# Sums of squares over each head's outputs: from one float32 product to two rounded ones, one gate panel later

## The chip, the cores and the metric

The kernel runs on one core of a Trainium2 chip. The metric is the device time of one execution in microseconds (us), lower is better; the time before is the median of three runs, and beside it stands one profiled execution whose trace is read here.

## What is computed

Two blocks follow each other on one sequence of 512 positions and 1024 features, in float32. The change is in the first block, in its recurrent branch (HGRN2) with 8 heads of 128 keys and 128 values. Cut to what matters:

```python
h = rmsnorm(x, norm_mix)
zu, zv, zq, zf, zi, zo, g_a, g_b = split(h @ w_in)
y_a = gmlp_branch(zu, zv, ...) @ w_up_a
# per head: S_t = diag(f_t) S_{t-1} + k_t v_t^T,  o_t = S_t^T q_t
o = hgrn2_chunkwise(silu(zq), sigmoid(-zf), zi, log_sigmoid(zf))
o = rmsnorm(o, norm_g) * silu(zo)        # per head, over its 128 values
x = x + (sigmoid(g_a) * y_a + sigmoid(g_b) * (o @ w_up_b)) @ w_out
```

The step that changes is the mean of o * o over the 128 values of a head, inside that `rmsnorm`. The rest (the feed-forward layers, the second block with its convolution, attention and feed-forward layers) is as it was.

## The kernel before, in words

**Layout.** Features lie on the 128 partitions and positions along the free dimension, so activations are tiles of 128x512. Each weight matrix is cut into panels of 128 output columns; there are 353 panels, and a hand-written list (`ORDER`) puts them in one sequence. A panel is loaded from HBM by the SP queue into `w_raw`, rounded by ScalarE into `w_hi` (`high`, L365), and GpSimd computes the rest `w_lo` = `w_raw` - `w_hi` (`low`, L348). Each is a ring of 3 panels. Activations are split in the same way into hi and lo. A product of one panel (`product`) is three matmuls of 128x128 by 128x512 for each of 8 feature tiles (L1268 to L1270: hi*hi, hi*lo, lo*hi), accumulated in a bank of PSUM, and VectorE evicts it (`scale_out`, L727, or `fill_out`), which counts `evicted` up. Panel p waits for its low part and for the eviction of panel p-2.

**Head stage.** It runs from about 40 to 410 us. Head h has six panels: p to p+3 are its forget gate, query, value and output gate, p+4 and p+5 are gate panels of the whole layer (`FILL`). The first head has four panels of another kind there. While TensorE multiplies the panels of head h, it does between them the small work of the head before, called `a` in the code: transposes, level scores, states and outputs (`turns`, `levels`, `chunk_kv`, `outputs`), the last into bank 7. Then ScalarE squares bank 7 into `o_sq` (L492), and `output_sums` multiplies 128x128 ones with `o_sq` in float32 into bank 2 (L1276), so that every partition holds the sum. ScalarE computes the inverse root of the mean in `root` (L378, L380), VectorE multiplies the outputs by it and by the gate (L1010, L1013), ScalarE rounds the result into `b_hi` (L368), and VectorE takes the rest into `b_lo` (L756). `b_hi[:, a]` and `b_lo[:, a]` are not used before that.

**The last head.** After head 7, a last turn (`last_head`, h is None) does the small work of head 7 between two gate panels and the first panels of `upa`, which have only four feature tiles, 12 matmuls.

**The order** on each engine is written out by hand: the functions `head` for ScalarE, VectorE and TensorE say what stands behind what, and semaphores join them. An engine works off its own list strictly in order, so an instruction that waits holds all behind it. In `head` of ScalarE the cast of panel p+6 stands ahead of `root`, then come the output gate's three activations (`log_sigmoid_part`), the split into `b_hi`, and the cast of panel p+7. In `head` of VectorE the eviction of panel p+4 stands ahead of the root's two products, and that of p+5 behind them.

**A form used elsewhere.** For the keys and queries of the second block the sums of squares are made with two rounded matmuls already, in `square_sums` (L1504, L1505), from `sq_hi` and `sq_lo`.

Of the kernel before, what the change touches and what calls it, by code (L numbers as in the profile page):

```python
# [8 lines left out]
P = 128  # L9
# [95 lines left out]
def build(nc, xT, panels, const, late, param, rows, ws, outT):  # L105
# [5 lines left out]
    with ctx:  # L111
        def sb(name, shape, dt=F):
            return ctx.enter_context(nc.sbuf_tensor(name, shape, dt))
# [21 lines left out]
        params = sb("params", [P, N_PARAM])  # L135
        q_gain = sb("q_gain", [P, 1])
        inv_rms = sb("inv_rms", [P, SEQ])
        arena = sb("arena", [P, ARENA])
# [114 lines left out]
        scores_clear = sem("scores_clear")  # L253
        spans_done, decays_done, queries_decayed = (sem(n) for n in ("spans_done", "decays_done", "queries_decayed"))
        o_made, o_squared, y_b, cum_done = sem("o_made"), sem("o_squared"), sem("y_b"), sem("cum_done")
        cum_keyed = sem("cum_keyed")
# [98 lines left out]
        def _(act):  # L355
# [55 lines left out]
            for m in range(DT):  # L411

                nc.scalar.activation(first_sq[:, m, :], x[:, m, :], ACT.Square).then_inc(squared, 1)
            act.wait_ge(c_in, 16)

            def gelu(t, panel):
# [24 lines left out]
            def head(h, a):  # L441
# [51 lines left out]
                if h is not None:  # L493
                    act.wait_ge(spans_done, h * 3 + 3)
                    nc.scalar.activation(qk[:, 6:, :], qk[:, 6:, :], ACT.Exp).then_inc(decays_done, 1)

                    nc.scalar.activation(qk[:, 1, :], cum[:, :], ACT.Exp)
                    nc.scalar.activation(chunk_decay[:, :], cum[:, P - 1:SEQ:P], ACT.Exp).then_inc(decays_done, 1)
                fill = FILL[h] if h is not None else FILL[HEADS_H][4:]
                high(p + 6)  # L500
                if h is None:
                    load_exp_and_log()
                if a is not None:
                    root(R_HEAD + a, ps[:, 2, :], 1.0 / P, o_inv[:, :])
                if h is not None:
                    act.wait_ge(evicted, p + 4)
                    log_sigmoid_part(z_o[:, :], silu_o[:, h % 2, :], o_log)
                if a is not None:
                    act.wait_ge(y_b, a + 1)
                    split(b_hi[:, a, :], o_tmp[:, :]).then_inc(hid_high, 1)  # L510
                for e in range(1, len(fill)):
                    high(p + 6 + e)

# [195 lines left out]
        def _(dve):  # L709
# [201 lines left out]
            def head(h, a):  # L911
# [80 lines left out]
                else:  # L992
                    fill_out(p + 2)
                if h in (1, 2):
                    for gr in (0, 1) if h == 1 else (2, 3):
                        gmlp_gate(gr)
# [7 lines left out]
                else:  # L1004
                    fill_out(p + 3)
                fill_out(p + 4)
                if a is not None:

# [5 lines left out]
                    low_hid(a + (HID_HEADS + 1), a, o_tmp[:, :], B)  # L1014
                for e in range(1, len(fill)):
                    fill_out(p + 4 + e)
                    if h == 0 and e == 1:
                        for gr in range(GROUPS):
                            gmlp_out(gr)
# [232 lines left out]
        def _(pe):  # L1252
# [148 lines left out]
            def output_sums(a):  # L1401
                pe.wait_ge(o_squared, a + 1)
                sums(2, c("ones"), o_sq[:, :])

# [3 lines left out]
            def head(h, a):  # L1408
# [26 lines left out]
                product(p + 4, a_hi, a_lo)  # L1435
                if a is not None:
                    output_sums(a)
                for e in range(1, len(FILL[h])):
                    product(p + 4 + e, a_hi, a_lo)
                    if h == 0 and e == 1:  # L1440
                        mix()

            def last_head(a):
# [292 lines left out]
```

## Time and profile before

| | us |
|---|---|
| median of three runs | 2079.77 (2077.23 to 2080.98) |
| the profiled execution | 2077.78 |
| its span, first to last instruction | 2076.0 |
| TensorE busy | 2047.2 (99% of the span), 9546 matmuls |
| VectorE busy | 971.0 (47%) |
| GpSimd busy | 853.0 (41%) |
| ScalarE busy | 785.9 (38%) |
| TensorE's granted clock | 0.998 of full speed |

The page gives the shares over the whole program. The stage of the heads is about a sixth of it. There the timelines of single engines are read: one line for each instruction or run of alike instructions, with start and duration in us, and in brackets the idle time ahead of it with what ended it. Matmuls overlap in the records: their distance from start to start is what one costs in a stream, and not the duration shown.

### The profile page before, as it was taken

The numbers are of one execution on the slowest core, as the hardware profiler recorded it, in microseconds if no ns is written. First come the engines' busy times: TensorE is split into PE (matmuls) and PEld (weight loads), VectorE is DVE, ScalarE is ACT, GpSimd is POOL, SyncE is SP. The second block draws the span as 40 slices with busy tenths as digits, with TensorE's granted clock in tenths as the row PEclk, the third lists the DMA queues.
The fourth block names the chain that finished last, engine by engine and source line by source line (L and its number), as shares of the span: only waits on it lengthen the run. The fifth ranks groups of instructions, "written<-read, shape, count | busy, mean of one in ns | idle before, by whom it ended". The sixth has DMA issues, their size and how long they took to land.

```text
span 2076.0 us, 23935 instructions
## 1 busy us (share of the span) xinstructions
PE 2047.2 (99%) x9546; PEld 1678.2 (81%) x9546; DVE 971.0 (47%) x1481; ACT 785.9 (38%) x1129; POOL 853.0 (41%) x357
## 2 busy tenths in 40 slices
PE   9899999999999999999999999999989999999999
PEld 6788888877888888888888888888867778888887
DVE  6688778524322313534453242453366655424243
ACT  5445544543222223522332222245366643222222
POOL 3333433454444444434444444454322234444444
PEclk9999999999999999999999999999999999999999
DMA  4222222242223232323223233232221122322323
GB/s 167 79 72 82 72 82 78 97 159 91 98 93 100 94 100 91 102 92 102 92 92 103 90 101 102 91 115 90 82 70 42 62 72 92 103 91 101 102 92 112
DMA packets 55120, 194.28 MB, mean 94 GB/s; under 512 B 6113, under 2 KB 6369, under 8 KB 55009
## 3 DMA queue, kind: packets, MB, share of 16 engines
q1 hardware_dynamic: 55008, 192.75, 28.4%
q8 instruction: 76, 1.25, 0.3%
q14 instruction: 36, 0.29, 0.0%
HBM read 190.62 MB, written 2.10 MB: 93 GB/s over the span
## 4 chain that ended last, share of the span: by engine, by line
PE 95%; DVE 3%; ACT 1%; issue 1%; DMA 0%; POOL 0%; SPq 0%; DVEq 0%; POOLq 0%
PE ps L1268 29%; PE ps L1270 29%; PE ps L1269 29%; PE ps L1374 1%; PE ps L1549 1%; PE ps L1582 1%; PE ps L1573 1%; PE ps L1293 1%; PE ps L1276 1%; DVE arena L899 0%; PE ps L1360 0%; PE ps L1396 0%; DMA x<-in_xT 0%; DVE a_lo L756 0%; PE ps L1398 0%
## 5 line engine op out<-in xcount | busy, mean ns | idle before, releaser
L348 POOL TENSOR_TENSOR w_lo<-w_raw,w_hi 128x1024 fp32r<-128x1024 f32 x353 | 852.8, 2419 | 1210.9 <-ACT w_hi L365 1205.2
L1268 PE MATMUL ps<-a_hi,w_hi 128*128 128x512 f32 x1472 | 583.5, 396 | 10.8 <-DVE a_lo L756 4.7
L1270 PE MATMUL ps<-a_hi,w_lo 128*128 128x512 f32 x1472 | 574.0, 390 | 0.0
L1269 PE MATMUL ps<-a_lo,w_hi 128*128 128x512 f32 x1472 | 573.6, 390 | 0.0
L365 ACT CAST w_hi<-w_raw 128x1024 fp32r<-128x1024 f32 x353 | 366.3, 1041 | 331.3 <-PE ps L1270 321.1
L1268 PE MATMUL ps<-b_hi,w_hi 128*128 128x512 f32 x1240 | 485.2, 391 | 2.5 <-DVE b_lo L756 2.2
L1270 PE MATMUL ps<-b_hi,w_lo 128*128 128x512 f32 x1240 | 482.6, 389 | 0.0
L1269 PE MATMUL ps<-b_lo,w_hi 128*128 128x512 f32 x1240 | 482.4, 389 | 0.0
L727 DVE TENSOR_TENSOR arena<-ps,inv_rms 128x512 f32<-128x512 f32 x208 | 143.4, 689 | 468.8 <-PE ps L1270 449.0
L1268 PEld LDWEIGHTS ps<-a_hi,w_hi 128*128 128x128 f32 x1472 | 276.9, 188 | 72.1 <-issue 11.9
L1270 PEld LDWEIGHTS ps<-a_hi,w_lo 128*128 128x128 f32 x1472 | 276.6, 188 | 58.6
L1269 PEld LDWEIGHTS ps<-a_lo,w_hi 128*128 128x128 f32 x1472 | 277.0, 188 | 58.0 <-issue 2.4
L1268 PEld LDWEIGHTS ps<-b_hi,w_hi 128*128 128x128 f32 x1240 | 232.8, 188 | 52.4 <-DVE b_lo L756 3.0
L1269 PEld LDWEIGHTS ps<-b_lo,w_hi 128*128 128x128 f32 x1240 | 232.8, 188 | 48.9 <-issue 1.0
L1270 PEld LDWEIGHTS ps<-b_hi,w_lo 128*128 128x128 f32 x1240 | 232.8, 188 | 48.5
L368 ACT ACTIVATE a_hi<-arena 128x512 fp32r<-128x512 f32 x70 | 43.6, 631 | 262.1 <-DVE arena L1047 125.7
L601 ACT ACTIVATE arena<-arena 128x512 f32<-128x512 f32 x44 | 27.8, 632 | 207.0 <-DVE arena L1091 207.0
L1133 DVE TENSOR_TENSOR x<-x,ps 128x512 f32<-128x512 f32 x40 | 27.5, 687 | 166.2 <-PE ps L1270 166.2
L756 DVE TENSOR_TENSOR a_lo<-arena,a_hi 128x512 fp32r<-128x512 f32 x70 | 50.0, 722 | 43.3 <-ACT a_hi L368 43.3
L1057 DVE TENSOR_TENSOR x<-x,ps 128x512 f32<-128x512 f32 x24 | 16.5, 687 | 107.7 <-PE ps L1270 107.7
L1121 DVE TENSOR_TENSOR arena<-arena 128x512 f32<-128x512 f32 x44 | 61.9, 1406 | 1.5
L388 ACT ACTIVATE arena<-arena 128x512 f32<-128x512 f32 x32 | 20.1, 628 | 93.3 <-DVE arena L727 93.3
(183 smaller groups left out, 1517.7 us busy)
## 6 DMA issues: line engine op xcount, KB each, us to landing
w_raw<-in_panels SPq DMA_DIRECT2D x353, 512.0 KB, 3.4
x<-in_xT SPq DMA_DIRECT2D x16, 256.0 KB, 2.9
outT<-x SPq DMA_DIRECT2D x8, 256.0 KB, 2.5
consts<-in_const SPq DMA_DIRECT2D x1, 528.5 KB, 7.8
arena<-in_rows SPq DMA_DIRECT2D x1, 256.0 KB, 4.5
arena<-in_ws SPq DMA_DIRECT2D x1, 256.0 KB, 4.8
consts<-in_late SPq DMA_DIRECT2D x1, 168.0 KB, 2.7
params<-in_param SPq DMA_DIRECT2D x1, 116.0 KB, 2.1
```

The source lines that it names most:

```text
L348: nc.gpsimd.tensor_tensor(w_lo[:, p % RING, :], w_raw[:, p % RING, :], w_hi[:, p % RING, :].bitcast(F), ALU.subtract).then_inc(w_low, 1)
L365: nc.scalar.copy(w_hi[:, p % RING, :], w_raw[:, p % RING, :]).then_inc(w_high, 1)
L368: return nc.scalar.activation(dst, src, ACT.Copy, scale=1.0 if scale is None else scale)
L601: nc.scalar.activation(conv_u[:, m % 2, :], conv_u[:, m % 2, :], ACT.Silu).then_inc(silu_done, 1)
L727: return v.tensor_tensor(dst, bank(p), inv_rms[:, :], ALU.mult)
L756: v.tensor_tensor(to[1][:, m, :], src, to[0][:, m, :].bitcast(F), ALU.subtract).then_inc(hid_low, 1)
L1121: v.tensor_tensor(conv_o[:, j, :], conv_u[:, j, :], conv_t[:, j, :], ALU.mult).then_inc(hid_raw, 1)
L1133: v.tensor_tensor(x[:, m, :], x[:, m, :], bank(p0 + m), ALU.add).then_inc(evicted, 1)
L1268: nc.tensor.matmul(o, wh, hi[:, kt, :], start=(kt == 0), stop=False)
L1269: nc.tensor.matmul(o, wh, lo[:, kt, :], start=False, stop=False)
L1270: ins = nc.tensor.matmul(o, wl, hi[:, kt, :], start=False, stop=(kt == tiles - 1))
L1276: nc.tensor.matmul(ps[:, bank_n, :], weights, src, start=True, stop=True).then_inc(sums_ready, 1)
```

## The change

It has four parts.

1. A second copy of the ones, `ones_r`, is made once by ScalarE as rounded values.
2. Behind the decays' activations, ScalarE rounds `o_sq` into `b_hi[:, a]`, and VectorE puts the rest, `o_sq` less that, into `b_lo[:, a]`, behind the decayed queries. Both tiles are overwritten later with the head's output, as before.
3. TensorE makes the sums from two matmuls with `ones_r`, and it makes them behind the second gate panel, p+5, where they stood ahead of it. In the last head they stay behind the third short panel.
4. On ScalarE the output gate's activations and the cast of panel p+7 now stand ahead of the root. On VectorE the eviction of panel p+5 stands ahead of the root's products.

```diff
+        ones_r = sb("ones_r", [P, P], R)
...
             act.wait_ge(c_in, 16)
+            split(ones_r[:, :], c("ones")).then_inc(ones_made, 1)
...
                     nc.scalar.activation(chunk_decay[:, :], cum[:, P - 1:SEQ:P], ACT.Exp).then_inc(decays_done, 1)
+                if a is not None:
+
+                    act.wait_ge(o_squared, a + 1)
+                    split(b_hi[:, a, :], o_sq[:, :]).then_inc(o_high, 1)
                 fill = FILL[h] if h is not None else FILL[HEADS_H][4:]
                 high(p + 6)
                 if h is None:
                     load_exp_and_log()
-                if a is not None:
-                    root(R_HEAD + a, ps[:, 2, :], 1.0 / P, o_inv[:, :])
                 if h is not None:
                     act.wait_ge(evicted, p + 4)
                     log_sigmoid_part(z_o[:, :], silu_o[:, h % 2, :], o_log)
-                if a is not None:
+                    for e in range(1, len(fill)):
+                        high(p + 6 + e)
+                if a is not None:
+                    root(R_HEAD + a, ps[:, 2, :], 1.0 / P, o_inv[:, :])
                     act.wait_ge(y_b, a + 1)
                     split(b_hi[:, a, :], o_tmp[:, :]).then_inc(hid_high, 1)
-                for e in range(1, len(fill)):
-                    high(p + 6 + e)
+                if h is None:
+                    for e in range(1, len(fill)):
+                        high(p + 6 + e)
...
                 else:
                     fill_out(p + 2)
+                if a is not None:
+                    dve.wait_ge(o_high, a + 1)
+                    v.tensor_tensor(b_lo[:, a, :], o_sq[:, :], b_hi[:, a, :].bitcast(F), ALU.subtract).then_inc(o_low, 1)
...
                 fill_out(p + 4)
+                if h is not None and a is not None:
+                    for e in range(1, len(fill)):
+                        fill_out(p + 4 + e)
                 if a is not None:
...
-                for e in range(1, len(fill)):
+                for e in range(1, len(fill) if h is None or a is None else 1):
                     fill_out(p + 4 + e)
...
             def output_sums(a):
-                pe.wait_ge(o_squared, a + 1)
-                sums(2, c("ones"), o_sq[:, :])
+                pe.wait_ge(ones_made, 1)
+                pe.wait_ge(o_low, a + 1)
+                nc.tensor.matmul(ps[:, 2, :], ones_r[:, :], b_hi[:, a, :], start=True, stop=False)
+                nc.tensor.matmul(ps[:, 2, :], ones_r[:, :], b_lo[:, a, :], start=False, stop=True).then_inc(sums_ready, 1)
...
                 product(p + 4, a_hi, a_lo)
-                if a is not None:
-                    output_sums(a)
                 for e in range(1, len(FILL[h])):
                     product(p + 4 + e, a_hi, a_lo)
                     if h == 0 and e == 1:
                         mix()
+                if a is not None:
+                    output_sums(a)
```

## Rows read from the trace of the kernel before

**Rows 1.** The page: its span, and the shares of the chain that ended last.

```profile
span 2076.0 us, 23935 instructions
PE 2047.2 (99%) x9546; PEld 1678.2 (81%) x9546; DVE 971.0 (47%) x1481; ACT 785.9 (38%) x1129; POOL 853.0 (41%) x357
...
PE 95%; DVE 3%; ACT 1%; issue 1%; DMA 0%; POOL 0%; SPq 0%; DVEq 0%; POOLq 0%
```

**Rows 2.** Waits of TensorE, 90 to 425 us: who, for whom, total us, times, longest.

```profile
PE ps L1268 <- POOL w_lo L348: 1.5, 1, 1.5
```

**Rows 3.** Timeline of TensorE, head 1, around its sums: start, us, engine, line, operation.

```profile
126.43 0.39 PE L1270 MATMUL ps<-a_hi,w_lo 128*128 128x512 f32 x1
126.66 1.02 PE L1276 MATMUL ps<-arena,consts 128*128 128x512 f32 x2
...
133.00 0.39 PE L1268 MATMUL ps<-a_hi,w_hi 128*128 128x512 f32 x1
```

**Rows 4.** Timeline of TensorE, the keys' sums in the second block.

```profile
1421.29 0.39 PE L1270 MATMUL ps<-b_hi,w_lo 128*128 128x512 f32 x1
1421.52 0.39 PE L1504 MATMUL ps<-gm_hi 128*128 128x512 f32 x1
...
1421.97 0.39 PE L1268 MATMUL ps<-b_hi,w_hi 128*128 128x512 f32 x1
```

**Rows 5.** Timeline of ScalarE, head 1, around the sums.

```profile
127.36 1.04 ACT L365 CAST w_hi<-w_raw 128x1024 fp32r<-128x1024 f32 x1
...
132.65 0.63 ACT L368 ACTIVATE b_hi<-arena 128x512 fp32r<-128x512 f32 x1 [1.15 <-DVE arena L1013]
133.19 1.98 ACT L365 CAST w_hi<-w_raw 128x1024 fp32r<-128x1024 f32 x2
```

**Rows 6.** Timeline of VectorE, head 1, to the next head's first eviction.

```profile
127.92 1.28 DVE L817 TENSOR_TENSOR x<-x 128x512 f32<-128x512 f32 x2
129.12 0.68 DVE L1003 TENSOR_TENSOR arena<-arena 128x512 f32<-128x512 f32 x1
129.73 0.68 DVE L727 TENSOR_TENSOR arena<-ps,inv_rms 128x512 f32<-128x512 f32 x1
...
131.10 1.52 DVE L1013 TENSOR_TENSOR arena<-arena 128x512 f32<-128x512 f32 x1
133.32 0.69 DVE L756 TENSOR_TENSOR b_lo<-arena,b_hi 128x512 fp32r<-128x512 f32 x1 [0.70 <-ACT b_hi L368]
...
138.72 0.69 DVE L727 TENSOR_TENSOR arena<-ps,inv_rms 128x512 f32<-128x512 f32 x1 [4.11 <-PE ps L1270]
```

**Rows 7.** Timelines of GpSimd, heads 1 and 2, and TensorE, head 2, first matmul of p+6.

```profile
128.47 3.59 POOL L348 TENSOR_TENSOR w_lo<-w_raw,w_hi 128x1024 fp32r<-128x1024 f32 x1 [6.73 <-ACT w_hi L365]
...
169.30 3.59 POOL L348 TENSOR_TENSOR w_lo<-w_raw,w_hi 128x1024 fp32r<-128x1024 f32 x1 [6.73 <-ACT w_hi L365]
...
173.74 0.39 PE L1268 MATMUL ps<-a_hi,w_hi 128*128 128x512 f32 x1
```

**Rows 8.** Timelines of GpSimd and TensorE, head 5: low part and first matmul of p+6.

```profile
291.50 2.42 POOL L348 TENSOR_TENSOR w_lo<-w_raw,w_hi 128x1024 fp32r<-128x1024 f32 x1 [6.73 <-ACT w_hi L365]
...
295.96 0.39 PE L1268 MATMUL ps<-a_hi,w_hi 128*128 128x512 f32 x1
```

**Rows 9.** Timelines of ScalarE, GpSimd and TensorE in the last head.

```profile
401.10 0.60 ACT L492 ACTIVATE arena<-ps 128x512 f32<-128x512 f32 x1 [3.63 <-PE ps L1398]
...
402.66 1.28 ACT L372 ACT_TABLE_LOAD   x1
404.74 0.69 ACT L378 ACTIVATE arena<-ps,consts 128x512 f32<-128x512 f32 x1 [0.80 <-PE ps L1276]
...
409.29 2.38 POOL L348 TENSOR_TENSOR w_lo<-w_raw,w_hi 128x1024 fp32r<-128x1024 f32 x1 [4.19 <-ACT w_hi L365]
...
411.71 0.50 PE L1268 MATMUL ps<-gm_hi,w_hi 128*128 128x512 f32 x1 [1.53 <-POOL w_lo L348]
412.05 0.39 PE L1269 MATMUL ps<-gm_lo,w_hi 128*128 128x512 f32 x1
```

More of the change, by code:

```diff
@@ L254, in build @@
         spans_done, decays_done, queries_decayed = (sem(n) for n in ("spans_done", "decays_done", "queries_decayed"))
+        ones_made, o_high, o_low = sem("ones_made"), sem("o_high"), sem("o_low")
         o_made, o_squared, y_b, cum_done = sem("o_made"), sem("o_squared"), sem("y_b"), sem("cum_done")
```

## The prediction

> **What bounds the kernel now.** I read the page first. TensorE is busy for 99% of the span, and 95% of the chain that ended last is its work, so the end moves by what TensorE's queue gains or loses and by nothing else [rows 1]. The change touches only the head stage, so I asked next who made TensorE wait between 90 and 425 us: one wait, 1.5 us, in the last head, for a weight panel's low part from GpSimd [rows 2]. In heads 1 to 7 TensorE never stands still, and 173.74 - 133.00 = 40.74 us pass from one head to the next [rows 3, 7]. VectorE, ScalarE and GpSimd have slack there; the question is how much of it lies behind each step that the change delays. For that I read the four engines' timelines around one head's sums, then the same for the other heads, then the last head, which has short products.
>
> I call a head's first panel p; p+4 and p+5 are its two gate panels, p+6 is the next head's first. All times below are those of the profiled execution, in us.
>
> **Part 1: the sums on TensorE.** Before, the last matmul of p+4 starts at 126.43, the float32 sums at 126.66 and the first matmul of p+6 at 133.00, with the 24 matmuls of p+5 between [rows 3]. A product's matmul costs 0.227 in the stream (three steps from 1421.29 to 1421.97, [rows 4]), so 24 take 5.44 and the sums 133.00 - 126.66 - 5.44 = 0.90. The new form is already in this kernel, for the keys: two rounded matmuls between products, 1421.52 to 1421.97, so 0.45 for the pair [rows 4]. That gives 0.90 - 0.45 = 0.45 per head, 3.6 over eight heads, if nothing else becomes late. The two waits ahead of the pair are like those ahead of the keys' pair, which run with no gap; the ones' rounding is one 128x128 activation in ScalarE's idle start, and I cost both at nothing (at most 0.3 once, if ScalarE were not idle there).
>
> **Part 2: what is added on ScalarE and VectorE.** Per head ScalarE gets one activation of 128x512 behind the decays' last Exp. Such a one stands at 132.65 with 0.63, and the next instruction starts 0.54 after it [rows 5]. It has its input long since, so it runs at 127.36, where the cast of panel p+6 started; that cast moves to 127.90 and its end to 128.94. VectorE gets one subtraction, which waits for it. The same pair in the kernel (ScalarE 132.65 + 0.63 = 133.28, VectorE 133.32) shows 0.04 between them [rows 5, 6]. The activation ends at 127.99, so the subtraction starts at 128.03, against 127.92, where the next VectorE instruction stood [rows 6]; with 0.61 from start to start of such instructions (129.12 to 129.73) everything behind it starts at 128.64, 0.72 later than before.
>
> **Part 3: GpSimd, which hides nothing here.** GpSimd computes the low part of panel p+6 from the cast. In head 1 that instruction shows 3.59 from 128.47, in head 5 2.42 from 291.50 [rows 7, 8]. The difference is VectorE: in heads 1 to 4 two extra instructions on SBUF data (gates, later low parts) and the one at L1003 run back to back from 127.92 to 129.80, and 128.47 + 3.59 = 132.06, GpSimd's end, is 2.42 after 129.64. So it could not begin before VectorE's last instruction with both inputs in SBUF was nearly done; the next one, an eviction out of PSUM at 129.73, did not hold it [rows 6, 7]. The reverse is at 131.10: VectorE's product shows 1.52 instead of 0.69, waiting for GpSimd to end [rows 6].
>
> The Trainium skill has this as a rule that speaks against the change ("SBUF — State Buffer", section "SBUF: two separate sides"): GpSimd and a VectorE instruction with two SBUF inputs exclude each other for a whole instruction. The trace agrees, with 3.59 against 2.42. Without such a rule the sum would be that of the first rival below.
>
> With the subtraction in front of them, the VectorE instructions that hold GpSimd end 0.72 later in heads 1 to 4, and the low part of p+6 is ready at 132.06 + 0.72 = 132.78. TensorE wants it 0.45 earlier than before, at 132.55. Before, the slack was 133.00 - 132.06 = 0.94 in head 1 and 173.74 - 172.89 = 0.85 in head 2 [rows 3, 7]; heads 3 and 4 show the same pattern with 0.88 and 0.87. With 0.03 from GpSimd's end to TensorE, the new wait is 0.45 + 0.72 + 0.03 less the slack: 0.26, 0.35, 0.32 and 0.33, together 1.26. A restart costs a little more: after the wait in the last head the second matmul starts 0.34 behind the first, not 0.227 [rows 9], about 0.12 each time, 0.48 in four. So **heads 1 to 4 lose 1.74** of what they gain. In heads 5 to 7 the slack is 295.96 - 293.92 = 2.04 [rows 8]; the cast ends at 291.96, GpSimd starts when L1003 is done, about 292.2, ends at 294.6, and TensorE wants it at 295.51. No wait.
>
> **Part 4: what is moved.** In heads 1 to 7 the sums start at 132.10, when p+5 is issued. Their input is ready at 128.72, over 3 us before. The eviction of p+5 now stands ahead of the root on VectorE, and on ScalarE the gate's three activations and the cast of p+7 do; these four are in at 131.8. Then root (0.68 + 0.63, from about 132.75), VectorE's two products (the second waits for GpSimd, which runs p+7 from 132.8 to 135.2, ends 135.8), split to 136.5, low part to 137.2. Next on VectorE is the next head's first eviction, possible at about 138.5 (138.72 before, [rows 6]): 1.3 to spare. The cast of p+8 stands behind the split and starts at 136.4 instead of 134.2; its low part ends at 139.9, and TensorE wants it only two panels later, after 148. SP's load of p+9 waits for the low part of p+6, 0.7 later, that of p+11 for the low part of p+8, 2.6 later; both are wanted in the middle of the next head, over 8 us behind their landing. The eviction of p+4, which p+6 needs, is done at 131.1, in time for 132.55. TensorE's transposes wait for the root to have read its bank, a whole panel behind it. All this I cost at nothing; the cover is the 4.11 us that VectorE stands idle before the next head's first eviction [rows 6], and the third rival says what it costs without it.
>
> **The last head** has products of 12 matmuls and the wait of 1.53 at 411.71, which ends with the low part begun at 409.29 [rows 9]. That waits for a cast which stands behind the root and the split on ScalarE. There the new activation (401.10 + 0.60 + 0.03 = 401.73, to 402.36) moves the cast of the fifth short panel and the table load behind it by 0.67; the load ends at 404.61 instead of 403.94 [rows 9]. The sums end 0.45 earlier, so the root starts at 404.63 instead of 404.74: **0.11 gained, not 0.45**. The sums' input is ready at 403.1, 0.6 before TensorE asks.
>
> **The sum.** 7 x 0.45 + 0.11 - 1.74 = 1.5. The profiled execution took 2077.78 in all, 1.78 around its span of 2076.0; it becomes 2076.3. The median of the runs shown, 2079.77, lies 2.0 above it. I forecast for the median: 2079.8 - 1.5 = **2078.2**. Bounds: 3.26 gained if no wait comes, 0 if the waits are double (3.5).
>
> **Rivals.**
> First, no wait for p+6. If GpSimd slips in between two VectorE instructions at 129.0, it ends at 131.4 and the gain is the full 3.26: 2076.5. For it: nothing in the trace; against it: asked at 128.47, it did not slip in, and so in four heads [rows 7]. It needs only 0.3 per head, though, and my times are good to 0.1 to 0.2.
> Second, the change doesn't do what it says: the pair costs as much as the single product, or other waits eat the gain, and the time stays at 2079.8. Against it the keys' pair [rows 4].
> Third, slower: the tail of the head gets into the next. If the low part of the head's output on VectorE comes after GpSimd has begun p+8 (137.4), it is held to 139.9, and the next head's first eviction goes from 138.5 to 140.5, 2.0 late. All of VectorE's head hangs on that eviction, up to GpSimd's p+6. Heads 2 to 4 would then wait 2.0 more each, heads 5 to 7, with 0.9 in hand, 1.1 each: 9.3, less the 1.5: 2087.6. It decides if that low part is later than the cast of p+8 by its end, so by some 0.9; on ScalarE the split stands ahead of that cast, which speaks against it.
>
> **Chances.** Forecast 0.67, first rival 0.16, second 0.10, third 0.07. A measurement of this kernel can tell about 0.2% (4.2 us) from no change. Neither the forecast nor the first two rivals reach that; the three runs shown spread by 3.75, so some chance of either sign is left for the measurement: faster 0.07, same 0.84, slower 0.09. The range takes the first rival and half of that spread below it, and the second above: 2074.9 to 2081.4.
>
> **What would show it.** Right: the pair's matmuls 0.45 apart from the next product; new waits of TensorE for GpSimd of about 0.3 at the first matmul of p+6 in heads 1 to 4 and none in heads 5 to 7; GpSimd's long instruction near 3.8 there; the distance of one head's sums to the next near 40.3 in heads 5 to 7; in the last head the wait longer than 1.53, by 0.3. Wrong: TensorE waiting for VectorE at the sums, or waits at p+6 in heads 5 to 7, or the next head's first eviction later behind p+6 than now.

## The result, and the profile after

| | before | after |
|---|---|---|
| median | 2080.38 us (2077.23 to 2081.38) | 2094.54 us (2093.41 to 2096.86) |
| ratio | | 1.0077, 95% interval 1.0065 to 1.0089 |
| profiled execution, its span | 2077.78, 2076.0 | 2096.86, 2095.1 |

The changed kernel is slower by 14.2 us by the medians and by 16 by the ratio. I had forecast 1.5 less. (The kernel before has one run more here than when I forecast, which moved its median from 2079.77 to 2080.38.) The page shows the loss in two of its parts, the span with the engines' busy time and the chain that ended last (compare [rows 1]):

```profile
span 2095.1 us, 23960 instructions
PE 2056.7 (98%) x9546; PEld 1685.1 (80%) x9546; DVE 990.2 (47%) x1489; ACT 791.1 (38%) x1138; POOL 851.0 (41%) x357
...
PE 87%; DVE 9%; issue 2%; ACT 1%; DMA 0%; POOL 0%; SPq 0%; DVEq 0%; POOLq 0%
```

TensorE's part of the chain fell from 95% to 87%, and VectorE's rose from 3% to 9%: TensorE waits for VectorE at places where it did not. The waits of TensorE between 90 and 445 us name the place (who, for whom, total us, times, longest):

```profile
PE ps L1283 <- DVE arena L736: 11.9, 4, 3.0
PE ps L1283 <- POOL w_lo L350: 1.8, 1, 1.8
```

The second line is the wait of the last head, where 1.5 stood [rows 2]. The first is new: four waits of 3 us at the first matmul of a product, each for an eviction by VectorE. TensorE's timeline in head 1 shows one, behind the new pair of matmuls (compare [rows 3]):

```profile
133.20 0.39 PE L1419 MATMUL ps<-b_hi,ones_r 128*128 128x512 f32 x1
133.43 0.40 PE L1420 MATMUL ps<-b_lo,ones_r 128*128 128x512 f32 x1
136.76 0.77 PE L1283 MATMUL ps<-a_hi,w_hi 128*128 128x512 f32 x1 [2.93 <-DVE arena L736]
137.32 0.63 PE L1284 MATMUL ps<-a_lo,w_hi 128*128 128x512 f32 x1
```

Panel p+6 was due at about 133.65 and starts at 136.76, 3.1 late. Then its matmuls are 0.43 apart instead of 0.23. The table of windows says why (us, busy time of PE, PEld, DVE, ACT, POOL, then the granted clock, the DMA share and GB/s):

```profile
136.70:140.00 3.30, 3.24 (x8) 2.59 (x9) 2.55 (x4) 1.37 (x2) 0.00 (x0) 0.51 0.39 144
140.00:143.50 3.50, 3.50 (x17) 2.89 (x16) 0.00 (x0) 0.20 (x1) 2.40 (x1) 1.00 0.00 0
```

Behind the wait of 3 us the clock is at the lower of its two levels, 1.2 GHz, for some 3 us. The first matmul behind p+6 starts at 143.78, so the product took 7.02 instead of 5.44. Head 1 therefore pays 3.1 + 1.6 = 4.7. Head 2 pays more: its p+6 is 3.15 late too, but the granted clock is 0.50 from 181.7 to 187.0.

What VectorE did instead of the eviction stands in its timeline, and beside it GpSimd's and ScalarE's (compare [rows 5 to 7]):

```profile
126.68 2.42 DVE L908 TENSOR_TENSOR arena<-arena 128x256 f32<-128x256 f32 x7
129.12 0.69 DVE L1005 TENSOR_TENSOR b_lo<-arena,b_hi 128x512 fp32r<-128x512 f32 x1
129.74 3.51 DVE L826 TENSOR_TENSOR x<-x 128x512 f32<-128x512 f32 x2
133.17 2.84 DVE L1015 TENSOR_TENSOR arena<-arena 128x512 f32<-128x512 f32 x1
135.94 1.27 DVE L736 TENSOR_TENSOR arena<-ps,inv_rms 128x512 f32<-128x512 f32 x2
...
130.11 2.58 POOL L350 TENSOR_TENSOR w_lo<-w_raw,w_hi 128x1024 fp32r<-128x1024 f32 x1 [7.25 <-ACT w_hi L367]
132.91 2.55 POOL L350 TENSOR_TENSOR w_lo<-w_raw,w_hi 128x1024 fp32r<-128x1024 f32 x1 [0.21 <-ACT w_hi L367]
...
128.47 0.62 ACT L370 ACTIVATE b_hi<-arena 128x512 fp32r<-128x512 f32 x1
128.99 1.04 ACT L367 CAST w_hi<-w_raw 128x1024 fp32r<-128x1024 f32 x1
...
131.80 1.03 ACT L367 CAST w_hi<-w_raw 128x1024 fp32r<-128x1024 f32 x1
```

Before, GpSimd's low part of p+6 showed 3.59, since it came behind VectorE's gates and L1003, and these three ran unhindered in 1.9. Now it shows 2.58: it got in between the two gates, and the second gate, held until GpSimd was done, makes 3.51 of the pair that took 1.28. (In heads 3 and 4 the GMLP's two low parts stand where heads 1 and 2 have the gates.) GpSimd then had its next job at once, the low part of p+7, because the cast of p+7 no longer stands behind the root (131.80 against 133.19 before, [rows 5]). It got in again ahead of L1015 (the old L1003), which shows 2.84 instead of 0.68. The eviction of p+4 stands behind all of this and came at 135.94. I had expected it at 130.4 and done by 131.1.

**Where the time went.** The distance of one head's sums to the next was 40.74 us everywhere. After, it is 44.97, 46.32, 45.15 and 45.05 from head 1 on, where VectorE has the extra instructions, and 40.33 in the two heads behind them. That is 17.7 more. Against 40.33 the first four lose 20.2, of which 12.5 are the late starts of p+6 and 7.6 the lower clock behind them; the pair's gain takes 2.5 off. The stretch before the first sums is 1.1 longer (the clock again, behind a wait of 3.4 us at 80 us that both kernels have), the last head 0.6 shorter, and a stretch of the second block, 1500 to 1661 us, 0.9 longer. Together 19.1, the difference of the two spans.

### The profile page after: what moved, and what is told of

Same layout as the page of the kernel before. It is cut to its first block, busy times and chain, and to the rows that moved or that the text cites. A ratio compares the mean times of both kernels' runs of the same rounds, so it can differ in the third digit from the quotient of the medians.

```text
span 2095.1 us, 23960 instructions
## 1 busy us (share of the span) xinstructions
PE 2056.7 (98%) x9546; PEld 1685.1 (80%) x9546; DVE 990.2 (47%) x1489; ACT 791.1 (38%) x1138; POOL 851.0 (41%) x357
## 4 chain that ended last, share of the span: by engine, by line
PE 87%; DVE 9%; issue 2%; ACT 1%; DMA 0%; POOL 0%; SPq 0%; DVEq 0%; POOLq 0%
PE ps L1283 27%; PE ps L1285 27%; PE ps L1284 27%; DVE arena L897 1%; PE ps L1566 1%; PE ps L1599 1%; PE ps L1590 1%; DVE arena L908 1%; PE ps L1389 1%; DVE arena L885 1%; DVE arena L850 1%; DVE arena L900 1%; DVE arena L736 0%; DVE arena L747 0%; DVE arena L1015 0%
## 5 line engine op out<-in xcount | busy, mean ns | idle before, releaser
L350 POOL TENSOR_TENSOR w_lo<-w_raw,w_hi 128x1024 fp32r<-128x1024 f32 x353 | 850.8, 2412 | 1232.0 <-ACT w_hi L367 1231.9
L610 ACT ACTIVATE arena<-arena 128x512 f32<-128x512 f32 x44 | 27.8, 632 | 207.0 <-DVE arena L1106 207.0
L370 ACT ACTIVATE b_hi<-arena 128x512 fp32r<-128x512 f32 x46 | 28.8, 627 | 92.5 <-DVE arena L1136 67.2
```

What stands on the lines that cost most here:

```text
L350: nc.gpsimd.tensor_tensor(w_lo[:, p % RING, :], w_raw[:, p % RING, :], w_hi[:, p % RING, :].bitcast(F), ALU.subtract).then_inc(w_low, 1)
L370: return nc.scalar.activation(dst, src, ACT.Copy, scale=1.0 if scale is None else scale)
L610: nc.scalar.activation(conv_u[:, m % 2, :], conv_u[:, m % 2, :], ACT.Silu).then_inc(silu_done, 1)
```

## The experiments

Two questions: what costs the time, and why GpSimd now gets in with the low part of p+6, which in the kernel before it never did. What it and VectorE compete for I call the port: in these traces GpSimd's subtraction and a VectorE instruction with two SBUF inputs take turns. GpSimd wins when it begins ahead of VectorE's next such instruction; its line then shows 2.4 to 2.6 us and that of VectorE 2.9. It loses when it begins only as the last of them ends; its line then shows 3 us and more, and no VectorE instruction is held. A measurement "in one run" rests on a single execution. All lines below are of head 1 unless said otherwise. L numbers shift by a few from kernel to kernel: the gates are L817 to L828, the last decayed query L1003 to L1017, `scale_out`, the eviction, L727 to L738, the low part on GpSimd L348 to L350.

### The order alone: e3_order_only

```diff
-                    split(b_hi[:, a, :], o_sq[:, :]).then_inc(o_high, 1)
...
-                    v.tensor_tensor(b_lo[:, a, :], o_sq[:, :], b_hi[:, a, :].bitcast(F), ALU.subtract).then_inc(o_low, 1)
...
-                nc.tensor.matmul(ps[:, 2, :], ones_r[:, :], b_hi[:, a, :], start=True, stop=False)
-                nc.tensor.matmul(ps[:, 2, :], ones_r[:, :], b_lo[:, a, :], start=False, stop=True).then_inc(sums_ready, 1)
+                pe.wait_ge(o_squared, a + 1)
+                sums(2, c("ones"), o_sq[:, :])
```

> The changed kernel with the sums as one float32 product again, without the rounding on ScalarE and the subtraction on VectorE: only the new order is left (sums behind p+5, cast of p+7 and eviction of p+5 ahead of the root). Theory A (the loss comes from GpSimd's request, which the added rounding moved into VectorE's gates): the request for p+6 falls where it fell before, GpSimd shows 3.59 us again, no wait at p+6, head distance 40.74 us, time that of before within 0.1%. Theory D (the new order by itself costs, by way of the cast of p+7 or of the later root): waits at p+6 or later ones, and over 1 us in each of heads 1 to 4.

Measured: 2078.32 against 2078.49 for the kernel before, ratio 1.0000 (0.9989 to 1.0011). The distance from head to head is 40.74, as before. Moving the sums, the root, the cast of p+7 and the eviction of p+5 costs nothing by itself. GpSimd's two low parts follow each other here too, but behind VectorE's run: 128.92, 5.93 for both, and no VectorE instruction was held.

### The rounding and the subtraction alone: e4_parts_only

```diff
+                    split(b_hi[:, a, :], o_sq[:, :]).then_inc(o_high, 1)
                 high(p + 6)
...
+                    dve.wait_ge(o_high, a + 1)
+                    v.tensor_tensor(b_lo[:, a, :], o_sq[:, :], b_hi[:, a, :].bitcast(F), ALU.subtract).then_inc(o_low, 1)
                 if h in (1, 2):
```

> The kernel before, with the rounding of the squares on ScalarE (ahead of the cast of p+6) and the subtraction on VectorE (ahead of the gates), neither of them used; the sums are the float32 product at its old place and the order of root, gate, casts and evictions is the old one. Theory R: the subtraction waits for the rounding, VectorE pauses, and GpSimd gets in: 2.6 us on GpSimd, 2.9 on the second gate, as in the changed kernel. The cast of p+7 is behind the root here, so there is no second hold; the eviction of p+4 is about 2.2 us later than it was, and TensorE waits 0.3 to 0.5 us at p+6 in heads 1 to 4: 1.5 to 3 us over the kernel before. My forecast's account (GpSimd is held until VectorE's run is over): low part of p+6 0.72 later, within the slack of 0.85 to 0.94, no wait, and the time of the kernel before within 0.5 us.

Measured: 2078.90 against 2077.66, ratio 1.0009 (0.9999 to 1.0018). VectorE and then GpSimd:

```profile
129.39 0.69 DVE L1001 TENSOR_TENSOR b_lo<-arena,b_hi 128x512 fp32r<-128x512 f32 x1
130.00 3.50 DVE L822 TENSOR_TENSOR x<-x 128x512 f32<-128x512 f32 x2
133.42 0.68 DVE L1011 TENSOR_TENSOR arena<-arena 128x512 f32<-128x512 f32 x1
...
130.37 2.58 POOL L349 TENSOR_TENSOR w_lo<-w_raw,w_hi 128x1024 fp32r<-128x1024 f32 x1 [7.24 <-ACT w_hi L366]
```

The two added instructions bring the first hold, 3.50 for the gates. The heads take 41.35 to 41.42 instead of 40.74 in heads 1 to 4, with waits of 0.3 to 0.4 for the eviction. That is 2.6 in sum, within the interval, which reaches from 0.2 us faster to 3.7 slower: the waits are shown by the trace, and the time by itself would not show them. My forecast's account, GpSimd behind the whole run and no wait, is refuted with nothing else of the change in place.

### The cast of p+7 put back behind the root: e2_cast_back

```diff
-                    for e in range(1, len(fill)):
-                        high(p + 6 + e)
...
-                if h is None:
-                    for e in range(1, len(fill)):
-                        high(p + 6 + e)
+                for e in range(1, len(fill)):
+                    high(p + 6 + e)
```

> The changed kernel with one part undone: ScalarE's cast of panel p+7 stands behind the root and the split again. Theory A: two holds make up the wait, GpSimd's low part of p+6 (holds the second gate) and that of p+7 (holds the product at L1015); only the first is left, the wait at p+6 falls from 2.9 to about 0.9 us in heads 1 to 4, and the time is about 2080.4 - 3.3 + 4 x 1.0 to 4 x 1.5, 2081 to 2083. Theory C (the first hold and the fall of TensorE's clock alone carry the loss): the wait stays above 2 us and the time above 2089.

Measured: 2076.59, and as much for the kernel before beside it, ratio 1.0003 (0.9991 to 1.0014). TensorE's new wait and VectorE's timeline:

```profile
PE ps L1280 <- DVE arena L733: 3.2, 4, 0.8
```

```profile
129.16 3.50 DVE L823 TENSOR_TENSOR x<-x 128x512 f32<-128x512 f32 x2
132.59 0.68 DVE L1012 TENSOR_TENSOR arena<-arena 128x512 f32<-128x512 f32 x1
```

The first hold is there, 3.50, and the second is gone, 0.68. The wait is 0.8 and not 3.0, and the matmul behind it follows 0.31 later, so the clock did not drop. Distances are 41.30 to 41.41. The time came out below what I had expected. Of the 14 to 16 us, one moved cast carries nearly all, though e3 shows that moved alone it is harmless. It needs the first hold in front of it.

### VectorE's extra work behind the eviction of p+4: e1_gates_behind

```diff
-                if h in (1, 2):
-                    for gr in (0, 1) if h == 1 else (2, 3):
-                        gmlp_gate(gr)
-                if h in (3, 4):
-                    for gr in (0, 1) if h == 3 else (2, 3):
-                        low_gmlp(gr)
...
                 fill_out(p + 4)
+                if h in (1, 2):
+                    for gr in (0, 1) if h == 1 else (2, 3):
+                        gmlp_gate(gr)
+                if h in (3, 4):
+                    for gr in (0, 1) if h == 3 else (2, 3):
+                        low_gmlp(gr)
```

> The changed kernel with one move: in heads 1 to 4 VectorE's two gate or low-part instructions and the eviction of panel p+4 change places, so that the eviction stands ahead of them. Theory A (port and order): GpSimd takes the SBUF port between two VectorE instructions and whatever VectorE has ahead of the eviction of p+4 is held for 2.4 us; with the eviction ahead of them TensorE's wait of 2.9 us at the first matmul of p+6 goes, the distance from one head's sums to the next is 40.3 us in all heads, and the time is the kernel before's 2080.4 less 3, about 2077.4. Theory B (the added rounding and subtraction themselves make VectorE late, wherever the gates stand): the waits stay near 2.9 us and the time stays above 2090.

Measured: 2072.26 against 2076.59, ratio 0.9974 (0.9965 to 0.9984). It beats both kernels. VectorE, GpSimd, TensorE:

```profile
127.32 0.68 DVE L1009 TENSOR_TENSOR arena<-arena 128x512 f32<-128x512 f32 x1
127.92 0.69 DVE L736 TENSOR_TENSOR arena<-ps,inv_rms 128x512 f32<-128x512 f32 x1
128.52 5.12 DVE L826 TENSOR_TENSOR x<-x 128x512 f32<-128x512 f32 x2
...
127.69 2.59 POOL L350 TENSOR_TENSOR w_lo<-w_raw,w_hi 128x1024 fp32r<-128x1024 f32 x1 [7.25 <-ACT w_hi L367]
130.49 2.61 POOL L350 TENSOR_TENSOR w_lo<-w_raw,w_hi 128x1024 fp32r<-128x1024 f32 x1 [0.21 <-ACT w_hi L367]
...
130.78 0.39 PE L1419 MATMUL ps<-b_hi,ones_r 128*128 128x512 f32 x1
131.24 0.40 PE L1283 MATMUL ps<-a_hi,w_hi 128*128 128x512 f32 x1
```

GpSimd is first twice and holds VectorE even longer, 5.12 for two gates, but nothing that TensorE needs soon stands behind them. TensorE goes from the pair into p+6 with no gap, and every head takes 40.33. From the end of head 1's p+4 to the first product of `upb` it is 2.98 us less than before.

### When GpSimd asks: e5_late_04, e7_late_368, e6_late_512

These leave the change away and only make ScalarE's cast of p+6, and so GpSimd's request, later, by an activation whose result is not used (4, 368 or 512 columns; the one of 512 is shown):

```diff
+                if h is not None and a is not None:
+                    split(b_hi[:, h, 0:512], inv_rms[:, :])
                 fill = FILL[h] if h is not None else FILL[HEADS_H][4:]
                 high(p + 6)
```

> The kernel before, with a ScalarE activation of 128x4 whose result nothing uses ahead of the cast of panel p+6 in heads 1 to 7: the cast and with it GpSimd's request come 0.1 us later, nothing else changes. In the kernel before GpSimd's instruction is shown from 0.05 us ahead of VectorE's second gate and loses; in the changed one it is shown from 0.24 us ahead and wins. Theory A (who is there first wins, and 0.1 us decides): with 0.1 us more it is too late for the second gate and 0.55 us ahead of VectorE's product at L1003, so it wins there: GpSimd shows about 2.6 us, not 3.59, and L1003 2.5 to 3 us, not 0.68, in heads 1 to 4; the eviction of p+4 moves to about 132, still ahead of TensorE's 133.0, so the time stays within 0.2% of before. Theory B: GpSimd shows 3.5 us and VectorE's instructions run back to back as before.

> The kernel before with an unused ScalarE activation of 128x368 ahead of the cast of p+6: GpSimd's request comes 0.42 us later, 0.37 us into a VectorE instruction, as in the changed kernel where GpSimd won. Requests at 0.55, 0.06 and 0.48 us into one lost. Theory P (the point within VectorE's instruction decides): GpSimd wins, shows about 2.6 us, and VectorE's L1005 shows 2.9 us in heads 1 to 4; TensorE waits for the eviction of p+4 by about 0.1 us or not at all, time as before within 0.2%. Theory R (VectorE's run decides: 26 instructions without a pause in the kernel before, one or two after its wait for the rounding in the changed kernel): GpSimd loses and shows about 3.2 us.

> As the kernel with the activation of 128x4, but with one of 128x512, as long as the rounding that the change adds: the request comes 0.54 us later, at about 129.01, 0.11 us ahead of VectorE's product at L1003. It lies between the 0.05 us that lost and the 0.24 us that won, so it places the edge: GpSimd near 3.1 us if VectorE wins, near 2.6 us with L1003 held if GpSimd wins. Theory A allows both and no stall of TensorE above 0.5 us; Theory B expects GpSimd at 3.1 us.

Measured in one run each: 2076.32, 2077.19, 2074.70, no change that one run can tell. GpSimd's line in e5, e7 and e6:

```profile
128.90 3.50 POOL L348 TENSOR_TENSOR w_lo<-w_raw,w_hi 128x1024 fp32r<-128x1024 f32 x1 [6.83 <-ACT w_hi L365]
```

```profile
128.43 3.20 POOL L348 TENSOR_TENSOR w_lo<-w_raw,w_hi 128x1024 fp32r<-128x1024 f32 x1 [7.13 <-ACT w_hi L365]
```

```profile
129.46 3.08 POOL L348 TENSOR_TENSOR w_lo<-w_raw,w_hi 128x1024 fp32r<-128x1024 f32 x1 [7.25 <-ACT w_hi L365]
...
128.38 1.28 DVE L819 TENSOR_TENSOR x<-x 128x512 f32<-128x512 f32 x2
129.59 0.68 DVE L1005 TENSOR_TENSOR arena<-arena 128x512 f32<-128x512 f32 x1
```

GpSimd lost each time, with the 3.5, 3.2 and 3.1 that its wait for the run's end gives, and always began some 0.14 before the end of the last VectorE instruction with two SBUF inputs: in e6 at 129.46 + 3.08 - 2.41 = 130.13, and L1005 ends at 130.27. (2.41 is what its instruction takes alone.) With these three and the kernel before, GpSimd has asked 0.06, 0.35, 0.48 and 0.56 us into a gate and lost each time. My first theory, that 0.1 us in the request decides who is first, fell here.

### The same from the other side: e8_after_late_4, e9_after_late_84

The changed kernel with the same unused activation, of 4 and of 84 columns.

> The changed kernel with an unused ScalarE activation of 128x4 behind the rounding: the request comes 0.10 us later, 0.48 us into the first gate. Theory P: GpSimd loses to the second gate and to L1015, shows about 3.3 us or more, and TensorE's wait at p+6 falls from 2.9 us to about 0.4 us for GpSimd: what I had forecast; time near 2078. Theory R: GpSimd wins as before, the waits stay near 2.9 us, time above 2088.

> As the one with 128x4, with 128x84: the request comes 0.19 us later, 0.56 us into the first gate, where the kernel before has it. Theory P: GpSimd loses to the second gate and L1015, shows 3.5 to 3.6 us, waits of TensorE for GpSimd of 0.3 to 0.5 us, time near 2078. Theory R: GpSimd wins at the second gate, waits near 2.9 us, time above 2088.

Measured in one run each: 2095.53 and 2097.61. GpSimd's first low part shows 2.48 and 2.43: it wins 0.47 and 0.54 us into the first gate, as it did at 0.38 in the changed kernel. Over the moments tried, which overlap, the kernel before always lost and the changed one always won; something else tells the two apart.

### A pause on VectorE: e11_pause_512

e6 with one wait more, and no instruction more on VectorE:

```diff
-                    split(b_hi[:, h, 0:512], inv_rms[:, :])
+                    split(b_hi[:, h, 0:512], inv_rms[:, :]).then_inc(probe, 1)
...
+                if h is not None and a is not None:
+                    dve.wait_ge(probe, h)
                 if h in (1, 2):
```

> The kernel before, with an activation of 128x512 on ScalarE ahead of the cast of panel p+6 in heads 1 to 7 (its result is not used), as in the run with the late request of 512 columns, and one addition to that: VectorE waits for this activation ahead of the gates. No instruction is added on VectorE; it pauses there for 0.02 to 0.1 us. Without that wait GpSimd was held, 3.08 us, and VectorE's instructions showed 0.68. Theory R: with the pause GpSimd gets in between, its low part shows 2.6, one VectorE instruction behind the request shows 2.9, in heads 1 to 4; the eviction of p+4 is then late and TensorE waits up to 0.5 us at p+6: 2 to 4 us over the kernel before. Theory S or any theory by the time of the request alone: no change against the run without the wait, 3.1 us on GpSimd, no wait of TensorE.

Measured: 2074.64 in one run. VectorE and GpSimd:

```profile
125.71 2.42 DVE L902 TENSOR_TENSOR arena<-arena 128x256 f32<-128x256 f32 x7
128.15 1.30 DVE L820 TENSOR_TENSOR x<-x 128x512 f32<-128x512 f32 x2
129.37 2.90 DVE L1008 TENSOR_TENSOR arena<-arena 128x512 f32<-128x512 f32 x1
...
129.14 2.58 POOL L349 TENSOR_TENSOR w_lo<-w_raw,w_hi 128x1024 fp32r<-128x1024 f32 x1 [7.25 <-ACT w_hi L366]
```

This is the pair that settles it. Against e6, where the gates start 0.07 before the decayed queries' recorded end, they start 0.02 behind it (125.71 + 2.42 = 128.13, 128.15). That is all VectorE loses, and it turns the outcome: GpSimd 2.58 instead of 3.08, VectorE's next instruction 2.90 instead of 0.68, in all of heads 1 to 4. The moment of the request can't be the cause: GpSimd asks 0.38 us into the second gate here, and at 0.35 into the same gate in e7 it lost. What the runs can't separate is the standstill itself from the semaphore wait that makes it, which VectorE reaches before it is met. I had expected 2 to 4 us more in the time. The eviction is late, but p+6 is due 0.45 later here than in the changed kernel, and the distances grow by at most 0.08.

### How long a pause is remembered: e12_pause_early

```diff
+                if h is not None and a is not None:
+                    split(b_hi[:, h, 0:512], inv_rms[:, :])
...
-                    decay_queries([1, 2, 3, 4])
+                    decay_queries([1, 2])
                     dve.wait_ge(decays_done, h * 4 + 3)
-                    decay_queries([5, 6, 7])
+                    decay_queries([3, 4, 5, 6, 7])
```

> The kernel before, with the same unused activation of 128x512 ahead of the cast of p+6, and VectorE's wait for the third group of decays moved ahead of the third decayed query (it stood ahead of the fifth), so that VectorE pauses some 0.6 us there and then runs five decayed queries, the two gates and the last decayed query without a pause. GpSimd asks in the first gate, five instructions and about 2.2 us behind the pause. Theory R says only that a run of 26 instructions loses nobody's place and one of 1 to 3 does; this run says on which side five lie: GpSimd held, over 3.0 us, if the pause has been forgotten by then, or 2.6 us with a VectorE instruction of 2.9 if it has not. A theory by the time of the request alone: held, as in all runs of the kernel before.

Measured: 2078.17 in one run. GpSimd's low part of p+6 in heads 3 and 4:

```profile
211.97 2.51 POOL L348 TENSOR_TENSOR w_lo<-w_raw,w_hi 128x1024 fp32r<-128x1024 f32 x1 [7.25 <-ACT w_hi L365]
...
253.31 3.72 POOL L348 TENSOR_TENSOR w_lo<-w_raw,w_hi 128x1024 fp32r<-128x1024 f32 x1 [7.25 <-ACT w_hi L365]
```

Five instructions and 2.1 us behind the pause GpSimd wins in heads 1 to 3 and loses in head 4, with instructions of the same shapes at the same distances. So at this distance it goes either way; behind 26 or 27 it always lost, behind one it always won.

The head stage of the kernel before has the short case too, and my forecast left it out. In each of heads 1 to 7 GpSimd's low part of p+3 asks one instruction behind a pause, and wins:

```profile
105.37 2.54 POOL L348 TENSOR_TENSOR w_lo<-w_raw,w_hi 128x1024 fp32r<-128x1024 f32 x1 [9.32 <-ACT w_hi L365]
...
105.59 2.60 DVE L876 TENSOR_TENSOR arena<-arena 128x256 f32<-128x256 f32 x1
```

One thing blurs the count of 26. Within that run GpSimd's low part of p+5 begins during an instruction out of PSUM, at 119.36, and holds L888 (119.61, 2.43 instead of 0.41). If a hold counts as a pause, only 17 instructions and 6.4 us lie between it and the request that lost. No request fell between about 3 and 6 us behind a pause or hold, so how far its effect reaches is open.

### The forecast's order: e10_sub_behind

The changed kernel with one line moved on VectorE, the subtraction behind the gates and the last decayed query, so that VectorE does not pause ahead of the gates:

```diff
-                if a is not None:
-                    dve.wait_ge(o_high, a + 1)
-                    v.tensor_tensor(b_lo[:, a, :], o_sq[:, :], b_hi[:, a, :].bitcast(F), ALU.subtract).then_inc(o_low, 1)
                 if h in (1, 2):
...
                     fill_out(p + 3)
+                if a is not None:
+                    dve.wait_ge(o_high, a + 1)
+                    v.tensor_tensor(b_lo[:, a, :], o_sq[:, :], b_hi[:, a, :].bitcast(F), ALU.subtract).then_inc(o_low, 1)
                 fill_out(p + 4)
```

> The changed kernel with one move: on VectorE the subtraction that makes the low part of the squares stands behind the gates (later heads: the GMLP's low parts) and behind the last decayed query, directly ahead of the eviction of panel p+4, where it stood ahead of the gates. The rounding on ScalarE, the pair of matmuls and all the rest are those of the changed kernel. Theory R (the run decides: GpSimd loses the SBUF port to a VectorE run that has gone on without a pause, and wins it one or two instructions behind a pause): the gates now follow the decayed queries without a pause, so GpSimd's low part of p+6 is held until the subtraction is nearly over, 3.7 us instead of 2.58; no VectorE instruction of the run shows 2.9; TensorE's waits at p+6 in heads 1 to 4 are 0.1 to 0.3 each, and the time is that of my forecast, 1 to 3 us below the kernel before. Theory S (the rounding ahead of the cast of p+6, that is the later request of GpSimd, decides): GpSimd wins as in the changed kernel, VectorE's eviction of p+4 comes late, heads 1 to 4 take 45 us each and the time stays near 2094.

Measured: 2073.59 against 2077.66, ratio 0.9978 (0.9969 to 0.9988). VectorE, GpSimd, TensorE:

```profile
126.42 1.28 DVE L826 TENSOR_TENSOR x<-x 128x512 f32<-128x512 f32 x2
127.63 0.68 DVE L1012 TENSOR_TENSOR arena<-arena 128x512 f32<-128x512 f32 x1
128.23 0.68 DVE L1017 TENSOR_TENSOR b_lo<-arena,b_hi 128x512 fp32r<-128x512 f32 x1
...
127.50 6.03 POOL L350 TENSOR_TENSOR w_lo<-w_raw,w_hi 128x1024 fp32r<-128x1024 f32 x2 [7.25 <-ACT w_hi L367]
...
130.81 0.40 PE L1420 MATMUL ps<-b_lo,ones_r 128*128 128x512 f32 x1
131.23 0.50 PE L1283 MATMUL ps<-a_hi,w_hi 128*128 128x512 f32 x1
131.56 0.39 PE L1284 MATMUL ps<-a_lo,w_hi 128*128 128x512 f32 x1
```

VectorE goes on without a gap, and GpSimd is held: the first of its two low parts ends at about 131.17 (the line of 6.03 holds both, the second takes 2.36), that is 3.67. TensorE starts p+6 at 131.23 where 131.04 was due, 0.19 late, and the matmul behind it takes 0.33. Heads 1 to 4 take 40.61 to 40.68, the others 40.33. By the two ratios, 1.0077 and 0.9978, one moved line is worth some 20 us to the changed kernel.

### What is left over

By their ratios, 0.9974 and 0.9978 of some 2077 us, e1 and e10 gained 5.4 and 4.6 us, and their heads explain 3.0 and 1.7 of it. (In its profiled execution e10 lost 1.6 of that again in the last head, where the granted clock was 0.84 from 410 to 418 us.) The rest lies where the code is the same. In the profiled executions the stretch before the end of head 1's p+4 is 1.3 and 1.5 shorter than in the kernel before. TensorE waits there for 3.4 us at about 80 in each of them, and the granted clock from 60 to 100 us is 0.96 before and 1.00 in e1 and e10.

The stretch of the second block (1500 to 1661 us before) takes 158.1 instead of 161.6. It also takes 158.1 in e6 and e11, kernels with the old sums, and 162.5 in the changed one. Here the same race decides. The kernel before, then e6:

```profile
1527.60 2.44 POOL L348 TENSOR_TENSOR w_lo<-w_raw,w_hi 128x1024 fp32r<-128x1024 f32 x1 [0.83 <-ACT w_hi L365]
1527.76 2.82 DVE L1143 TENSOR_TENSOR gm_hi<-arena,gm_hi 128x512 fp32r<-128x512 f32 x1
1530.73 0.77 PE L1504 MATMUL ps<-gm_hi 128*128 128x512 f32 x1 [2.61 <-DVE gm_hi L1143]
```

```profile
1528.04 3.09 POOL L348 TENSOR_TENSOR w_lo<-w_raw,w_hi 128x1024 fp32r<-128x1024 f32 x1 [0.82 <-ACT w_hi L365]
1528.21 0.68 DVE L1145 TENSOR_TENSOR gm_hi<-arena,gm_hi 128x512 fp32r<-128x512 f32 x1
```

GpSimd asks 2.2 us and three instructions behind a pause of VectorE. Before, it wins, and TensorE waits 2.61 us for the instruction that it holds; in e6 it loses, and that wait is gone. The stretch is 2.1 us longer where GpSimd wins and TensorE's clock stays up (e7), and 3.5 where the clock falls as well (before). Over the 14 traces GpSimd wins in six (before, after, e3, e7, e8, e9) and loses in eight (e1, e2, e4, e5, e6, e10, e11, e12), and e6 and e7, which differ only in the length of an unused activation in the head stage, fall on different sides. At a second such place, 466.84 before, three instructions and 2.4 us behind a pause, it wins in 13 of 14 (2.37) and loses once, in e1 at 462.54, there to the next instruction alone (2.96). So at 2.1 to 2.4 us the outcome is open each time. Whether e1 and e10 lose this race in every execution, or only in the one profiled, no run here shows; that much of their gain, up to 3.5 us, is not shown to be theirs.

## Why the prediction was wrong

**What bounds the kernel** held: only TensorE's queue moved the end, and the change acted in the head stage alone.

**Part 1** held in mechanism and nearly in size: undisturbed heads went from 40.74 to 40.33, a gain of 0.41 for 0.45.

**Part 2** held in its numbers. The cast starts 0.52 behind the rounding (0.54 forecast), the subtraction 0.03 behind its end. But it stopped at the number. I wrote that the subtraction would start at 128.03, against 127.92, and took this for a shift. It is a wait, by which VectorE stands still for 0.02 to 0.1 us in a run of 26 instructions, and e11 shows that such a pause alone changes who gets the port.

**Part 3 is the step that failed.** It took from [rows 7] that GpSimd comes behind the whole run of VectorE's two-input instructions, and carried that over to the changed kernel. The trace shows it only for a request 26 instructions behind VectorE's last pause. In the changed kernel the request comes one instruction behind the new pause, and GpSimd shows 2.58 where I had 3.8, the second gate 2.9, and TensorE waits 2.9 to 3.0 for the eviction of p+4 in four heads, where I had 0.26 to 0.35 for GpSimd. With the run unbroken the step is right to 0.1: e10 has 3.67 on GpSimd (3.8 forecast) and losses of 0.28 to 0.35 per head (0.38 to 0.47 forecast).

The page of the Trainium skill that I named ("SBUF — State Buffer", section "SBUF: two separate sides") says that whichever starts first holds the port pair for its whole instruction. That agrees with the runs, 2.90 on a VectorE instruction and 3.59 on GpSimd, and I read only half of it: it works against VectorE as much as against GpSimd. That section doesn't say who is first when GpSimd asks within a VectorE run.

**The first rival** had the right mechanism, GpSimd slipping in between two VectorE instructions, at a chance of 0.16. Its price was wrong even in sign. I counted what GpSimd gains and not what VectorE loses: 2.2 for the gate, with the eviction of p+4 queued behind it, which p+6 needs. "For it: nothing in the trace" was wrong too. [rows 6] has L1013 held at 1.52 by GpSimd, the same exclusion with GpSimd first, and at 105.37 and 119.36, in the same head, GpSimd slipped into VectorE's work and held an instruction for 2 us.

**Part 4** costed the cast of p+7 at nothing, because its own consumers had time. It said that GpSimd would run p+7 from 132.8; that GpSimd then has a second job ready when the first is done, and takes the port from VectorE once more, was not asked. The eviction of p+4, "done at 131.1, in time for 132.55", rested on Part 3 and came at 135.94. e2 sizes this term: without the moved cast the wait is 0.8, with it 3.0, and only behind 3.0 did the clock fall. A restart, which I had priced at 0.12, cost 1.6 in head 1 and 2.9 in head 2 with it.

**The last head** held: the wait grew from 1.53 to 1.80 (1.87 forecast). **The third rival**, slower by the head's tail, did not happen: VectorE's next first eviction still has 4.07 of idle time ahead of it, as against 4.11 [rows 6]. Slower it was, by a mechanism of which the first rival had one half and no rival the other.

Two sums are off by little. 2079.77 less 1.52 is 2078.25, and half of the spread of 3.75 on either side gives a range of 2074.6 to 2081.6. The measured time lies outside of either.

## What to carry to other kernels

Where GpSimd and VectorE share the SBUF port, price both outcomes of the race, and for VectorE ask what is queued behind the instruction that would be held. A wait that costs next to nothing can change the winner. Put evictions that TensorE needs ahead of optional two-input work; e1 made the outcome irrelevant that way, which is safer than e10's way of deciding it. And a cast moved early doesn't only hand its consumer data early, it starts GpSimd early, on the port of another engine.

## What the runs showed of the hardware

- GpSimd's request lost behind 26 and 27 VectorE instructions without a pause, at every moment tried (six kernels), and won one instruction behind a pause of 0.02 us (2.58 us, with a VectorE instruction of 2.9). At three to five instructions and 2.1 to 2.4 us it went either way. What in VectorE's queue makes the difference no run here shows.
- When GpSimd loses, it begins about 0.14 us before the recorded end of VectorE's last two-input instruction; a VectorE instruction out of PSUM does not hold it.
- Waits of TensorE of 0.2 to 0.8 us left its clock at full speed; behind the one of 3.1 in head 1 it was granted 0.51 for 3.3 us. In between it went either way: at full speed behind 1.8 us in e1's last head and 2.6 in e7's second block, down behind 1.8 in e10's last head and 2.6 in the kernel before's second block.
